# Depthwise convolution of a hybrid trunk kernel: two of four channel tiles as 32-column matmuls, and half of the softmax scaling on VectorE

## The chip, the cores and the metric

One core of one Trainium2 chip. The metric is the device time of one execution in microseconds (us). Engines are named as in the profile: PE is TensorE, PEld its weight loads, DVE is VectorE, ACT is ScalarE, POOL is GpSimd, SP is the engine that issues most DMAs.

## The reference

A two-layer trunk over 384 tokens (128 context tokens, then 256 latent tokens) of width 1024. Each layer is a half-step SwiGLU FFN, token mixing, a half-step SwiGLU FFN. The change touches only the token mixing of layer 0, the even mixer:

```python
q, k, v, a = split(h @ w_in)
q, k = rms_norm(q), rms_norm(k)            # rotary on latent tokens
attn = block_attention(q, k, v)            # 8 heads, 2 key/value heads, head size 64
glu  = a[..., :512] * sigmoid(a[..., 512:])
conv = silu(layer_norm(depthwise_conv(glu, conv_w, conv_b)))   # 31 taps, 512 channels
return concatenate([attn, conv]) @ w_out
```

The depthwise convolution gives each of 512 channels its own 31 weights: out[channel, n] is the sum over k of w[channel, k] times glu[channel, n + k - 15]. Context tokens attend to 128 keys, latent tokens to 384.

## The kernel before

Channels stand on the 128 partitions, tokens run along the free dimension (`TOK` = 384). A weight unit is 128 x 2048 f32 (1 MB); SP loads it into a ring of four, ACT makes its rounded high part (L515), DVE the rest (L837), and PE multiplies it in three passes, high by high, high by low, low by high (L1357 to L1359). FFNs take most of the time. A second ring, `m_raw`, carries 128 x 1024 rows of the modulation weights during the FFNs; in the even mixer it is idle.

The order of work is written out by hand, one program per engine, tied together by semaphores. In the even mixer the 512 convolution channels are four tiles `j` of 128 (`CT` = 4). `glu_mul(j)` on DVE writes the gated input of a tile into `padded[:, j, :]`, with zeros around both token groups, so that one tap is a multiplication of 399 columns (`CONV_N`) shifted by k. The parts that matter:

- **Taps on DVE.** `taps(j, k0, k1)` (L1111 for the first tap, L1115 for the others) adds one tap after the other into `conv[:, j, :]`; each waits for the one before it in the same tile. Tile 0 is done during the projections, tile 1 has 9 taps there and the rest later, tile 2 and 6 taps of tile 3 come in the attention loop, five taps a step, taken in turn from two tiles (`more_taps`).
- **Taps on PE.** The other 25 taps of tile 3 are matmuls (`conv_taps`, L1660) of a 128 x 128 diagonal matrix of weights by 399 columns of `padded`, summed in PSUM bank 1. ACT makes each diagonal (`tap_diags`, L647).
- **The attention loop** has 12 steps `m` (`PAIR_STEPS`): pairs of heads by three token blocks. Every third step, m = 0, 3, 6, 9, is a context block with 128 keys, the others are latent blocks with 384. I call them narrow and wide steps. In a step, PE makes the scores (L1671), DVE takes the maximum (L1193) and its scaled negative (L1195), ACT the exponential and its sum for both heads (L726), DVE the reciprocal (L1200), ACT scales the probabilities of both heads (L736), PE transposes them (`flip`, L1683), ACT copies them out of PSUM (`flipped_copy`, L716), and PE multiplies them by the values (L1694). After every third step a pair of heads is complete: ACT writes its high part (`mix_high`, L706) and DVE its low part (`mix_low`, L1204).
- **The orders in a step m.** PE: `scores(m + 2)` (waits for the exponential of m), taps, `values(m - 1)` (waits for the copies of m - 1), `flip(m)` (waits for the scaled probabilities of m). ACT: exponential of m, `mix_high` when due, the copies of m - 1, the scaling of m, one tap diagonal while there are any. DVE: reciprocal of m, `mix_low` when due, the maximum of m + 1, five taps.
- After the loop DVE adds the four tiles' sums into `conv_sum()` (L1235 to L1241), from which PE takes the mean for the layer norm (L1715), beside the output projection of the attention half (`proj_out`). That projection begins right after the last `values`.

Of the kernel before, what the change touches and what calls it, by code (L numbers as in the profile page):

```python
# [26 lines left out]
P = 128  # L27
# [22 lines left out]
DVE_TILES = CT - 1  # L50
DIAGS = 21
LAST_DVE_TAPS = 6
# [124 lines left out]
def build(nc, cache_k, cache_v, c, c_ctx, sgu_w, sgu_b, k_ident, k_rope, k_fourier, w_units, w_pairs, w_rows,  # L177
          x_cols, cond_cols, cols_a, cols_b, conv_cols, sgu_rows, y_cols, new_cache_k, new_cache_v):
    ctx = ExitStack()
    with ctx:  # L180
# [22 lines left out]
        conv_wt = sb("conv_wt", [P, CT, CONV_K])  # L203
        cond = sb("cond", [P, KT, COND_ROWS])
        cond_raw = sb("cond_raw", [P, 2 * KT])
        mod_pick = sb("mod_pick", [P, 2])
# [30 lines left out]
        tap_diag = sb("tap_diag", [P, DIAGS, P], stack=r)  # L237
        padded = sb("padded", [P, CT, PAD_N], stack=r)
# [82 lines left out]
        diag_ready, tap_used = sem("diag_ready"), sem("tap_used")  # L321
# [22 lines left out]
        def conv_sum():  # L344

            return rot[:].rearrange("p a b -> p (a b)")[:, 0:CONV_N]
# [7 lines left out]
        def row_products():  # L354
            return mod_rows(TRING + 2)

# [5 lines left out]
        def _(sp):  # L362
# [16 lines left out]
            def load_ffn(s):  # L379
                u0, n = UNIT0[s], TILE0[s]  # L380

                if s == 0:
# [8 lines left out]
                    for dst, src in ((vec_b[:], cols_b), (conv_wt[:], conv_cols)):  # L391
                        sp.dma_start(dst, src).then_inc(vectors_in, 16)
# [42 lines left out]
            for n in range(5, M0_UNITS):  # L435
                load_unit(u + n)
            load_ffn(2)
# [24 lines left out]
        def _(pool):  # L462
# [22 lines left out]
            pool.wait_ge(e_zero, 4)  # L485
            def add_channel_squares(m, sq):
# [16 lines left out]
        def _(act):  # L503
# [138 lines left out]
            def tap_diags(k0, k1):  # L642

                for k in range(k0, k1):
                    if k >= DIAGS + LAST_DVE_TAPS:
                        act.wait_ge(tap_used, k - DIAGS - LAST_DVE_TAPS + 1)
                    nc.scalar.activation(tap_diag[:, k % DIAGS, :], ident[:], ACT.Copy,  # L647
                                         scale=conv_wt[:, CT - 1, k:k + 1]).then_inc(diag_ready, 1)
# [22 lines left out]
            tap_diags(LAST_DVE_TAPS, LAST_DVE_TAPS + 6)  # L671
# [16 lines left out]
            tap_diags(LAST_DVE_TAPS + 6, LAST_DVE_TAPS + DIAGS)  # L688
# [29 lines left out]
            for m in range(PAIR_STEPS):  # L718
# [106 lines left out]
        def _(dve):  # L825
# [232 lines left out]
            nc.vector.tensor_reduce(mod_pick[:], ident[:].rearrange("p (a b) -> p b a", a=4)[:, 0:2, :], axis=AX.X,  # L1058
# [39 lines left out]
            dve.wait_ge(vectors_in, 32)  # L1098
# [34 lines left out]
            dve.wait_ge(vectors_in, 32)  # L1133
# [43 lines left out]
            taps(1, 0, 2)  # L1177
# [4 lines left out]
            taps(1, 2, 9)  # L1182
# [23 lines left out]
            last = CT - 1  # L1206
            rest = [1, 2] * (CONV_K - 9) + [2, last] * LAST_DVE_TAPS + [2] * (9 - LAST_DVE_TAPS)
            at = {1: 9, 2: 0, last: 0}

            def more_taps(n):  # L1210

                for j in rest[:n]:
                    taps(j, at[j], at[j] + 1)
                    at[j] += 1
                del rest[:n]

            dve.wait_ge(glu_done, 3)
            split(u + 8)
            more_taps(6)
# [11 lines left out]
            assert not rest  # L1231

            dve.wait_ge(conv_done, DVE_TILES)
            dve.wait_ge(dve_self, tap_at[last])
            a = mark(nc.vector.tensor_tensor(conv_sum(), conv[:, 0, :], conv[:, 1, :], ALU.add))  # L1235
            dve.wait_ge(tap_used, CONV_K - LAST_DVE_TAPS)
            b = mark(nc.vector.tensor_tensor(conv[:, last, :], conv[:, last, :], ps[:, 1, 0:CONV_N], ALU.add))
            dve.wait_ge(dve_self, a)
            dve.wait_ge(dve_self, mark(nc.vector.tensor_tensor(conv_sum(), conv_sum(), conv[:, 2, :], ALU.add)))
            dve.wait_ge(dve_self, b)  # L1240
            nc.vector.tensor_tensor(conv_sum(), conv_sum(), conv[:, last, :], ALU.add).then_inc(conv_summed, 1)  # L1241
# [110 lines left out]
        def _(pe):  # L1352
# [69 lines left out]
            def mod_columns(k):  # L1422
# [4 lines left out]
                for q in range(PAIR_TILES):  # L1427
                    ins = mm(ps[:, 7, 2 * q:2 * q + 2], mod_part[:, k % 2, q * P:(q + 1) * P], mod_pick[:], start=True, stop=True)
# [223 lines left out]
            tap = [LAST_DVE_TAPS]  # L1652

            def conv_taps(n):

                for k in range(tap[0], min(tap[0] + n, CONV_K)):
                    pe.wait_ge(diag_ready, k - LAST_DVE_TAPS + 1)
                    if k == LAST_DVE_TAPS:
                        pe.wait_ge(glu_done, CT)
# [229 lines left out]
```

## Time and profile before

| | |
|---|---|
| median of 3 runs | 1400.91 us (1400.43 to 1401.33) |
| the profiled execution, its own time | 1400.48 us |
| its span, first to last instruction | 1398.6 us |
| PE busy | 1383.6 us, 99% |
| DVE busy | 982.6 us, 70% |
| ACT busy | 566.0 us, 40% |
| POOL busy | 43.0 us, 3% |

The span is what the rows of the trace cover; the execution's own time is 1.9 us longer. Busy time is a mean over stages, and an engine with idle time in one stage can be the bound of the next, so the stage that changes has to be looked at by itself.

### The profile page before, as it was taken

What the parts mean: (1) busy time and instruction counts of PE and PEld (TensorE: products, weight loads), DVE (VectorE), ACT (ScalarE), POOL (GpSimd) and SP (SyncE); (2) the same over time, 40 slices, a digit from 0 to 9 for tenths busy, and PEclk for the clock granted to TensorE, in tenths of its full rate; (3) what the DMA queues carried; (4) which work ended last, traced back from release to release, by engine and by line L of the source; (5) the groups of instructions that cost most, each with busy time, mean ns of one, the idle gap of its engine ahead of it and who ended that gap; (6) DMA issues with size and microseconds to landing.
All of it is one profiled execution on the core that took longest, in us unless ns stands there. A gap on an engine that the chain in (4) does not pass through costs nothing.

```text
span 1398.6 us, 21118 instructions
## 1 busy us (share of the span) xinstructions
PE 1383.6 (99%) x8057; PEld 1347.5 (96%) x8057; DVE 982.6 (70%) x1502; ACT 566.0 (40%) x797; POOL 43.0 (3%) x48
## 2 busy tenths in 40 slices
PE   7999999999999999999999999999999999999999
PEld 6999999999958999999999999999999999999999
DVE  5788879849896988788338888787385488444422
ACT  4433332236586643333226333332365363333320
POOL 0000000010001200000002000000010110000000
PEclk8999999999999999999999999999999999999999
DMA  9865567533301365564334666574333253333331
GB/s 378 311 232 213 210 231 262 198 121 104 114 11 61 142 250 212 222 230 177 120 122 179 225 230 230 215 243 166 133 121 143 91 210 122 132 136 135 136 122 74
DMA packets 46373, 243.53 MB, mean 174 GB/s; under 512 B 5616, under 2 KB 8304, under 8 KB 25712
## 3 DMA queue, kind: packets, MB, share of 16 engines
q1 hardware_dynamic: 46032, 242.68, 48.0%
q8 instruction: 34, 0.56, 0.2%
q14 instruction: 19, 0.16, 0.0%
q10 hardware_dynamic: 288, 0.13, 0.0%
HBM read 241.09 MB, written 1.70 MB: 174 GB/s over the span
## 4 chain that ended last, share of the span: by engine, by line
PE 95%; DVE 3%; ACT 1%; issue 0%; DMA 0%; SPq 0%; DVEq 0%; ACTq 0%
PE ps L1357 30%; PE ps L1359 30%; PE ps L1358 30%; DVE conv L1115 1%; PE ps L1660 1%; PE ps L1814 0%; PE ps L1434 0%; PE ps L1765 0%; PE ps L1766 0%; PE ps L1767 0%; PE ps L1789 0%; DMA x<-in_x_cols 0%; DVE smax L1193 0%; PE ps L1418 0%; DVE n_full L915 0%
## 5 line engine op out<-in xcount | busy, mean ns | idle before, releaser
L1357 PE MATMUL ps<-a_hi,w_hi 128*128 128x384 f32 x1584 | 532.9, 336 | 0.5 <-DVE a_lo L923 0.4
L1358 PE MATMUL ps<-a_lo,w_hi 128*128 128x384 f32 x1584 | 529.6, 334 | 0.0
L1359 PE MATMUL ps<-a_hi,w_lo 128*128 128x384 f32 x1584 | 529.6, 334 | 0.0
L837 DVE TENSOR_TENSOR w_lo<-w_raw,w_hi 128x2048 fp32r<-128x2048 f32 x153 | 350.6, 2293 | 190.7 <-ACT w_hi L515 190.7
L515 ACT ACTIVATE w_hi<-w_raw 128x2048 fp32r<-128x2048 f32 x153 | 291.9, 1909 | 245.3 <-DMA w_raw<-in_w_units 245.1
L1357 PEld LDWEIGHTS ps<-a_hi,w_hi 128*128 128x128 f32 x1584 | 297.6, 188 | 6.4 <-issue 3.0
L859 DVE SCALAR_TENSOR_TENSOR m_raw<-m_raw 128x1024 f32<-128x1024 f32 x256 | 299.3, 1220 | 0.0
L1358 PEld LDWEIGHTS ps<-a_lo,w_hi 128*128 128x128 f32 x1584 | 297.7, 188 | 0.1
L1359 PEld LDWEIGHTS ps<-a_hi,w_lo 128*128 128x128 f32 x1584 | 297.6, 188 | 0.0
L1359 PE MATMUL ps<-h_hi,w_lo 128*128 (+1 forms) x704 | 236.6, 336 | 0.0
L1357 PE MATMUL ps<-h_hi,w_hi 128*128 (+1 forms) x704 | 236.5, 336 | 0.0
L1358 PE MATMUL ps<-h_lo,w_hi 128*128 (+1 forms) x704 | 236.5, 336 | 0.0
L594 ACT ACTIVATE glu<-ps 128x384 f32<-128x384 f32 x82 | 40.2, 491 | 282.0 <-PE ps L1359 282.0
L1359 PEld LDWEIGHTS ps<-h_hi,w_lo 128*128 128x128 f32 x704 | 132.4, 188 | 0.0
L1357 PEld LDWEIGHTS ps<-h_hi,w_hi 128*128 128x128 f32 x704 | 132.3, 188 | 0.0
L1358 PEld LDWEIGHTS ps<-h_lo,w_hi 128*128 128x128 f32 x704 | 132.3, 188 | 0.0
L1002 DVE TENSOR_TENSOR glu<-glu,ps 128x384 f32<-128x384 f32 x82 | 45.1, 550 | 75.4 <-ACT glu L594 75.4
L596 ACT ACTIVATE h_hi<-glu 128x384 f32 (+1 forms) x82 | 43.1, 526 | 131.0 <-DVE glu L1002 131.0
L1005 DVE TENSOR_TENSOR h_lo<-glu,h_hi 128x384 f32 (+1 forms) x82 | 45.8, 559 | 66.5 <-ACT h_hi L596 66.5
L541 ACT ACTIVATE a_hi<-n_full,m_shift 128x128 fp32r<-128x128 f32 x96 | 42.4, 455 | 43.9 <-DVE n_full L915 43.9
L1115 DVE SCALAR_TENSOR_TENSOR conv<-padded,conv_wt,conv 128x399 f32<-128x399 f32 x95 | 56.5, 631 | 1.3
L896 DVE SCALAR_TENSOR_TENSOR x<-ps,m_gate,x 128x128 f32<-128x128 f32 x96 | 34.6, 412 | 26.5 <-PE ps L1359 26.4
(193 smaller groups left out, 859.0 us busy)
## 6 DMA issues: line engine op xcount, KB each, us to landing
w_raw<-in_w_units SPq DMA_DIRECT2D x153, 1024.0 KB, 4.9
m_raw<-in_w_rows SPq DMA_DIRECT2D x128, 512.0 KB, 5.7
m_raw<-in_w_pairs SPq DMA_DIRECT2D x5, 1024.0 KB, 13.5
p_raw<-in_w_pairs SPq DMA_DIRECT2D x3, 1024.0 KB, 24.5
x<-in_x_cols SPq DMA_DIRECT2D x2, 768.0 KB, 5.3
out<-x SPq DMA_DIRECT2D x8, 192.0 KB, 1.9
fourier<-in_k_fourier SPq DMA_DIRECT2D x1, 768.0 KB, 8.1
m_raw<-in_c_ctx SPq DMA_DIRECT2D x1, 512.0 KB, 9.0
```

The source lines that it names most:

```text
L515: nc.scalar.activation(w_hi[:, slot(u), :], w_raw[:, slot(u), :], ACT.Copy).then_inc(hi_done, 1)
L541: nc.scalar.activation(a_hi[:, d, lo:hi], n_full[:, d, lo:hi], ACT.Identity, bias=m_shift[:, n, d, cnd:cnd + 1]).then_inc(a_hi_done, 1)
L594: nc.scalar.activation(glu[:, 0, :], ps[:, 2 * b, 0:TOK], ACT.Silu).then_inc(silu_done, 1)
L596: nc.scalar.activation(h_hi[:, bass.ds(t + RING * i, 1), :], glu[:], ACT.Copy).then_inc(h_hi_done, 1)
L837: nc.vector.tensor_tensor(w_lo[:, slot(u), :], w_raw[:, slot(u), :], w_hi[:, slot(u), :].bitcast(FP32), ALU.subtract).then_inc(lo_done, 1)
L859: nc.vector.scalar_tensor_tensor(out, mod_rows(n % TRING), 1.0, cond_row(cnd), ALU.mult, ALU.mult, accum_out=mod_cols[:, bass.ds(FIRST_TIL ...
L1002: nc.vector.tensor_tensor(glu[:, 0, :], glu[:, 0, :], ps[:, 2 * b + 1, 0:TOK], ALU.mult).then_inc(prod_done, 1)
L1005: nc.vector.tensor_tensor(h_lo[:, bass.ds(t + RING * i, 1), :], glu[:], h_hi[:, bass.ds(t + RING * i, 1), :].bitcast(FP32), ALU.subtract). ...
L1115: ins = nc.vector.scalar_tensor_tensor(conv[:, j, :], padded[:, j, k:k + CONV_N], conv_wt[:, j, k:k + 1], conv[:, j, :], ALU.mult, ALU.add)
L1357: mm(out, whi, mhi, start=start, stop=False)
L1358: mm(out, whi, mlo, start=False, stop=False)
L1359: return mm(out, wlo, mhi, start=False, stop=stop)
```

## The change

- Tiles 1 and 3 of the convolution go to PE completely; tiles 0 and 2 stay on DVE. PE takes four taps at a time (a quad; 8 quads a tile, the 32nd tap has weight zero). For that the input of the tile is copied by 16 DMAs into two free slots of `m_raw`: partition 32 k + c of group g holds channel 32 g + c shifted by k columns. A matmul with a 128 x 32 weight (four diagonals of 32, one above the other) then sums four taps of 32 channels. Four such matmuls, one for each group, fill the 128 partitions of the result (`conv_quads_of`).
- POOL makes all these weights once per tile before the attention (`quad_w`), ACT's diagonals (`tap_diags`) go away, and ACT takes each finished tile out of PSUM with its bias (`quad_evict`, in steps 4 and 11).
- In the attention loop PE has 4 quads ahead of the first step and then 1, 1, 1, 1, 0, 2, 1, 1, 1, 1, 1, 1 of them. DVE has tile 2 alone: 7 taps ahead of the loop, three a step for m < 3, then two.
- The probabilities of a step's first head are scaled on ACT as before, those of the second on DVE (`scale_second`), between the reciprocal and `mix_low` or the next maximum. `flip` waits for each half separately.
- The sums of the four tiles are added in another order: two additions in step 10, one after the loop. They stand in `padded[:, 0]` instead of `rot`.
- SP: 16 DMAs behind the loads of units 8 and 10 of this mixer. One small load of weights (`quad_wt`) at the start; DVE waits for three vector loads instead of two. `mod_pick` has 32 columns instead of 2.

```diff
-DVE_TILES = CT - 1
-DIAGS = 21
-LAST_DVE_TAPS = 6
+COND_GROUP = 32
+DVE_TILES = 2
+QUADS = 8
+GROUPS = 4
+PAD_W = PAD_N + 1
+QUAD_N = PAD_W - (P // COND_GROUP - 1)
...
+        def quad_x(i):
+            return m_raw[:, i, 0:GROUPS * QUAD_N].rearrange("p (g n) -> p g n", g=GROUPS)
+
+        def quad_w(i):
+            return m_raw[:, 2, i * UNIT // 2:(i + 1) * UNIT // 2].rearrange("p (q c) -> p q c", c=COND_GROUP)
...
             for n in range(5, M0_UNITS):
                 load_unit(u + n)
+                if n not in QUAD_LOAD:
+                    continue
+                i = QUAD_LOAD.index(n)
+                j = QUAD_TILES[i]
+                sp.wait_ge(glu_done, j + 1)
+                for k in range(P // COND_GROUP):
+                    for g in range(GROUPS):
+                        sp.dma_start(quad_x(i)[k * COND_GROUP:(k + 1) * COND_GROUP, g, :],
+                                     padded[g * COND_GROUP:(g + 1) * COND_GROUP, j, k:k + QUAD_N]).then_inc(quad_in[i], 16)
...
+            for i in range(CT - DVE_TILES):
+                nc.gpsimd.tensor_tensor(quad_w(i),
+                                        mod_pick[:].unsqueeze(1).to_broadcast([P, GROUPS * QUADS, COND_GROUP]),
+                                        quad_wt[:, i].rearrange("p g q -> p (g q)").unsqueeze(2)
+                                        .to_broadcast([P, GROUPS * QUADS, COND_GROUP]), ALU.mult).then_inc(quad_ready, 1)
...
-            def tap_diags(k0, k1):
...
+            def quad_evict(i):
+                j = QUAD_TILES[i]
+                act.wait_ge(quad_used, QUADS * (i + 1))
+                nc.scalar.activation(conv[:, j, :], ps[:, 1, 0:CONV_N], ACT.Identity,
+                                     bias=vec_b[:, B_CONV_B + j:B_CONV_B + j + 1]).then_inc(quad_out, 1)
...
                 act.wait_ge(rec_done, m + 1)
-                for h in range(2):
-                    n = 2 * m + h
-                    ins = nc.scalar.activation(probs(m)[:, h, 0:width(m)], probs(m)[:, h, 0:width(m)], ACT.Copy,
-                                               scale=srec[:, n:n + 1])
-                ins.then_inc(prob_done, 1)
-                k = LAST_DVE_TAPS + DIAGS + m
-                tap_diags(k, min(k + 1, CONV_K))
+                nc.scalar.activation(probs(m)[:, 0, 0:width(m)], probs(m)[:, 0, 0:width(m)], ACT.Copy,
+                                     scale=srec[:, 2 * m:2 * m + 1]).then_inc(prob_done, 1)
+                if m in QUAD_OUT:
+                    quad_evict(QUAD_OUT.index(m))
...
+            def scale_second(m):
+                width = CTX if m % TT == 0 else LAT + PAST
+                dve.wait_ge(rec_done, m + 1)
+                nc.vector.tensor_scalar(probs(m)[:, 1, 0:width], probs(m)[:, 1, 0:width], srec[:, 2 * m + 1:2 * m + 2], None,
+                                        ALU.mult).then_inc(half_scaled, 1)
...
             for m in range(PAIR_STEPS):
                 reciprocals(m)
+                scale_second(m)
                 if m >= 4 and (m - 4) % TT == 0:
                     mix_low((m - 4) // TT, ps[:, 0, 0:TOK])
                 if 1 <= m < PAIR_STEPS - 1:
                     attention(m + 1)
-                more_taps(5)
...
+                k = 7 + 2 * m + min(m, 3)
+                taps(2, min(k, CONV_K), min(k + 2 + (m < 3), CONV_K))
+                if m == PAIR_STEPS - 2:
+                    dve.wait_ge(conv_done, DVE_TILES)
+                    a = mark(nc.vector.tensor_tensor(conv_sum(), conv[:, 0, :], conv[:, 2, :], ALU.add))
+                    dve.wait_ge(dve_self, a)
+                    dve.wait_ge(quad_out, 1)
+                    a = mark(nc.vector.tensor_tensor(conv_sum(), conv_sum(), conv[:, 1, :], ALU.add))
...
+            def conv_quads_of(n):
+
+                for k in range(quad[0], quad[0] + n):
+                    i, q = k // QUADS, k % QUADS
+                    if q == 0:
+                        pe.wait_ge(quad_in[i], 16 * GROUPS * (P // COND_GROUP))
+                        pe.wait_ge(quad_ready, i + 1)
+                        if i:
+                            pe.wait_ge(quad_out, i)
+                    for g in range(GROUPS):
+                        ins = mm(ps[g * COND_GROUP:(g + 1) * COND_GROUP, 1, 0:CONV_N], quad_w(i)[:, g * QUADS + q, :],
+                                 quad_x(i)[:, g, 4 * q:4 * q + CONV_N], start=q == 0, stop=q == QUADS - 1)
+                    ins.then_inc(quad_used, 1)
+                quad[0] += n
...
             scores(0)
             scores(1)
-            conv_taps(3)
+            conv_quads_of(QUADS_AT[0])
             for m in range(PAIR_STEPS):
                 if m + 2 < PAIR_STEPS:
                     scores(m + 2)
-                conv_taps(2 if m < PAIR_STEPS - 2 else 1)
+                conv_quads_of(QUADS_AT[1 + m])
...
+QUADS_AT = [4, 1, 1, 1, 1, 0, 2, 1, 1, 1, 1, 1, 1]
+QUAD_OUT = [4, 11]
+QUAD_TILES, QUAD_LOAD = [1, 3], [8, 10]
```

## Rows read from the trace of the kernel before

**Rows 1.** The page: the chain that ended last, by engine.

```profile
PE 95%; DVE 3%; ACT 1%; issue 0%; DMA 0%; SPq 0%; DVEq 0%; ACTq 0%
```

**Rows 2.** Projections and loop: stretch, length, busy PE, PEld, DVE, ACT, POOL; clock, DMA.

```profile
316.00:381.30 65.30, 65.30 (x381) 63.22 (x380) 57.97 (x91) 38.18 (x67) 1.76 (x4) 1.00 0.31 106
381.30:428.67 47.37, 43.44 (x268) 23.81 (x267) 44.26 (x98) 39.03 (x107) 0.00 (x0) 1.00 0.07 23
```

**Rows 3.** The chain within 381 to 429 us, by line.

```profile
by line: DVE conv L1115 33.2%; PE ps L1660 17.5%; DVE smax L1193 8.6%; PE ps L1683 6.8%; PE ps L1671 6.2%; PE ps L1694 6.0%; ACT prob_t L716 3.4%; issue 2.4%; ACT e_sig L736 2.1%; DVE a_lo L1204 2.1%; DVE smaxn L1195 2.0%; ACT e_sig L726 1.
```

**Rows 4.** Timeline of DVE, steps 4 and 5: start, us, instruction, count, idle before.

```profile
398.46 0.56 DVE L1204 TENSOR_TENSOR a_lo<-ps,a_hi 128x384 fp32r<-128x384 f32 x1
398.94 0.95 DVE L1193 TENSOR_REDUCE smax<-ps 128x2 f32<-128x768 f32 x1
399.92 0.16 DVE L1195 SCALAR_TENSOR_TENSOR smaxn<-smax,stat_row 128x2 f32<-128x2 f32 x1
400.00 2.81 DVE L1115 SCALAR_TENSOR_TENSOR conv<-padded,conv_wt,conv 128x399 f32<-128x399 f32 x5
402.73 0.16 DVE L1200 RECIPROCAL srec<-ssum 128x2 f32<-128x2 f32 x1
402.80 0.40 DVE L1193 TENSOR_REDUCE smax<-ps 128x2 f32<-128x256 f32 x1
```

**Rows 5.** Timeline of ACT in steps 2 to 5, and the end of step 10's exponentials.

```profile
391.26 1.12 ACT L736 ACTIVATE prob<-prob,srec 128x384 f32<-128x384 f32 x2
392.29 0.39 ACT L647 ACTIVATE tap_diag<-ident,conv_wt 128x128 f32<-128x128 f32 x1
392.58 0.44 ACT L726 ACTIVATE e_sig<-ps,smaxn,stat_row 128x128 f32<-128x128 f32 x1
...
397.31 0.21 ACT L726 ACTIVATION_READ_ACCUMULATOR prob<-ps,smaxn,stat_row 128x1 f32 x1
...
400.12 0.67 ACT L726 ACTIVATE e_sig<-ps,smaxn,stat_row 128x384 f32<-128x384 f32 x1 [0.35 <-DVE smaxn L1195]
...
401.34 0.20 ACT L726 ACTIVATION_READ_ACCUMULATOR e_sig<-ps,smaxn,stat_row 128x1 f32 x1
401.43 0.86 ACT L716 ACTIVATE prob_t<-ps 128x384 f32<-128x384 f32 x2
...
419.96 0.20 ACT L726 ACTIVATION_READ_ACCUMULATOR prob<-ps,smaxn,stat_row 128x1 f32 x1
```

**Rows 6.** Timeline of PE in step 5.

```profile
401.59 0.92 PE L1671 MATMUL ps<-kdup,qk 64*128 64x384 f32 x4 [0.19 <-ACT e_sig L726]
402.43 1.61 PE L1660 MATMUL ps<-padded,tap_diag 128*128 128x399 f32 x4
403.97 0.88 PE L1694 MATMUL ps<-prob_t,v_nat 128*64 128x128 f32 x12
404.78 0.88 PE L1683 MATMUL ps<-ident,e_sig 128*128 128x128 f32 x6
```

**Rows 7.** Timeline of PE at the kernel's start: matmuls with 32 weight columns.

```profile
31.44 1.07 PE L1418 MATMUL ps<-p_raw,cond 128*32 128x256 f32 x16
32.44 0.44 PE L1357 MATMUL ps<-a_hi,w_hi 128*128 128x384 f32 x1
```

**Rows 8.** DVE: two scaling groups by form, and taps of one tile alone.

```profile
L1298 DVE TENSOR_SCALAR o_v<-o_v,stat 128x512 f32<-128x512 f32 x3 | 1.3, 482 | 0.0
...
L1259 DVE TENSOR_SCALAR e_diag<-ident,stat 128x128 f32<-128x128 f32 x3 | 0.7, 285 | 0.0
...
368.71 4.65 DVE L1115 SCALAR_TENSOR_TENSOR conv<-padded,conv_wt,conv 128x399 f32<-128x399 f32 x7
```

**Rows 9.** POOL's additions (min/median/max ns), a 64 KB issue on SP, landing times.

```profile
L492 POOL TENSOR_TENSOR qk_sq<-qk_sq x3: 1015/1020/2873, 433.7 to 437.9; 128x384 f32<-128x384 f32 x3
...
326.03 0.65 SPq L434 DMA_DIRECT2D v_nat<-in_cache_v  x1
...
bs<-in_sgu_b SPq DMA_DIRECT2D x4, 64.0 KB, 8.1
```

More of the change, by code:

```diff
@@ L203, in build @@
         conv_wt = sb("conv_wt", [P, CT, CONV_K])
+        quad_wt = sb("quad_wt", [P, CT - DVE_TILES, GROUPS, QUADS])
         cond = sb("cond", [P, KT, COND_ROWS])
         cond_raw = sb("cond_raw", [P, 2 * KT])
-        mod_pick = sb("mod_pick", [P, 2])
+        mod_pick = sb("mod_pick", [P, COND_GROUP])
         mod_part = sb("mod_part", [P, 2, PAIR])
@@ L320, in build @@
         mix_hi, mix_ready = sem("mix_hi"), sem("mix_ready")
-        diag_ready, tap_used = sem("diag_ready"), sem("tap_used")
+        quad_in = [sem(f"quad_in{i}") for i in range(CT - DVE_TILES)]
+        quad_ready, quad_used, quad_out, half_scaled = (
+            sem(n) for n in ("quad_ready", "quad_used", "quad_out", "half_scaled"))
         ln_mean_done, ln_xc, ln_sq, ln_stat, ln_ms, ln_root, ln_diag, ln_bc, ln_y = (
@@ L390, in load_ffn @@
                     load_unit(u0 + 2)
[L391 removed]
+                    for dst, src in ((vec_b[:], cols_b), (conv_wt[:], conv_cols), (quad_wt[:], conv_quads)):
                         sp.dma_start(dst, src).then_inc(vectors_in, 16)
@@ L1204, in mix_low @@
                 nc.vector.tensor_tensor(a_lo[:, j, :], src, a_hi[:, j, :].bitcast(FP32), ALU.subtract).then_inc(mix_ready, 1)
[L1206 to L1215, printed above, removed]
+            split(u + 8)
             dve.wait_ge(glu_done, 3)
-            split(u + 8)
-            more_taps(6)
+            taps(2, 0, 7)
             glu_mul(3)
@@ L1229, in _ @@
                     attention(m + 1)
-                more_taps(5)
[L1231 to L1237, printed above, removed]
+                k = 7 + 2 * m + min(m, 3)
[6 more added lines that the diff above has]
+                    a = mark(nc.vector.tensor_tensor(conv_sum(), conv_sum(), conv[:, 1, :], ALU.add))
             dve.wait_ge(dve_self, a)
-            dve.wait_ge(dve_self, mark(nc.vector.tensor_tensor(conv_sum(), conv_sum(), conv[:, 2, :], ALU.add)))
-            dve.wait_ge(dve_self, b)
-            nc.vector.tensor_tensor(conv_sum(), conv_sum(), conv[:, last, :], ALU.add).then_inc(conv_summed, 1)
+            dve.wait_ge(quad_out, 2)
+            nc.vector.tensor_tensor(conv_sum(), conv_sum(), conv[:, 3, :], ALU.add).then_inc(conv_summed, 1)
             mix_low(QT - 1, ps[:, 0, 0:TOK])
@@ L1427, in mod_columns @@
                 for q in range(PAIR_TILES):
-                    ins = mm(ps[:, 7, 2 * q:2 * q + 2], mod_part[:, k % 2, q * P:(q + 1) * P], mod_pick[:], start=True, stop=True)
+                    ins = mm(ps[:, 7, 2 * q:2 * q + 2], mod_part[:, k % 2, q * P:(q + 1) * P], mod_pick[:, 0:2], start=True, stop=True)
                 ins.then_inc(cols_done, 1)
@@ L1650, in _ @@
             pe.wait_ge(e_tc, 2)
[L1652 to L1659, printed above, removed]
-                    mm(ps[:, 1, 0:CONV_N], tap_diag[:, k % DIAGS, :], padded[:, CT - 1, k:k + CONV_N], start=k == LAST_DVE_TAPS,
-                       stop=k == CONV_K - 1).then_inc(tap_used, 1)
-                    tap[0] = k + 1
+            quad = [0]
+            def conv_quads_of(n):
[11 more added lines that the diff above has]
+                quad[0] += n
             def scores(m):
@@ L1679, in flip @@
                 for h in range(2):
+                    if h:
+                        pe.wait_ge(half_scaled, m + 1)
+                    else:
+                        pe.wait_ge(prob_done, m + 1)
                     if m:
@@ L1709, in _ @@
             values(PAIR_STEPS - 1)
-            assert tap[0] == CONV_K
+            assert quad[0] == QUADS * (CT - DVE_TILES)
             def means(src, at):
@@ L1877 @@
     named["sgu_rows"] = np.ascontiguousarray(np.concatenate([vectors["sgu_norm_g"], vectors["sgu_norm_b"]]))
+    taps = np.zeros((QUADS * 4, CONV_CH), np.float32)
+    taps[:CONV_K] = np.asarray(inputs["conv_w"])[0]
+    quads = taps.reshape(QUADS, 4, CT, GROUPS, COND_GROUP).transpose(1, 4, 2, 3, 0).reshape(P, CT, GROUPS, QUADS)
+    named["conv_quads"] = np.ascontiguousarray(quads[:, QUAD_TILES])
     arrays, args = {}, []
```

26 lines of the change are left out of this document (9 added, 17 removed).

## The prediction

> **What bounds the kernel now.** I read the page first. Its chain by engine [rows 1] shows a kernel that is PE from end to end, so work taken from DVE or ACT is worth something only where PE waits for them. I looked for that place next, with the busy times by stretch [rows 2]. In the projections, 316 to 381.3 us, PE is busy for all of 65.3 us: the 9 taps of tile 1 and the diagonals that leave that stretch give nothing back. In the attention loop, 381.3 to 428.67 us, PE has 3.9 us without work and DVE is busy for 44.3 of 47.4 us. The chain within it [rows 3] has DVE's taps as its largest line, a third, with the maximum behind them, and PE's taps second. So the loop is set by DVE, and PE is not far behind.
>
> The timelines give the loop's pace. The exponentials of step 4 end at 397.52 and those of step 10 at 420.16 [rows 5]: 22.6 us for six steps, 11.3 for three. DVE's five taps take 2.73 us a step, 402.73 minus 400.00 [rows 4], 8.2 for three; three reciprocals (0.07 each), two wide and one narrow maximum with its negative (1.06 and 0.52, from 398.94 to 400.00 and from 402.80 and the next 0.12) and `mix_low` (0.48) are 3.3. Together 11.5, the whole pace: DVE has no gap. PE, by the starts of step 5 [rows 6]: scores 0.84, taps 1.54, values 0.81, flip 0.81, 4.0 us for a wide step and about 2.7 for the narrow one, 10.7 for three.
>
> **The change, part by part.**
>
> *Taps leave DVE.* Two instead of five a step. They are now of one tile, and seven in a row of one tile stand 0.66 apart (4.65 / 7) [rows 8] against 0.55 in turn. Two cost 1.3 us. They stand behind the maximum of m + 1 and are hidden by the exponentials of m + 1, which take 1.42 us (400.12 to 401.54) [rows 5]. Behind a narrow one (0.97: two halves, each shorter by 0.67 - 0.44 = 0.23) 0.3 us stick out.
>
> *Scaling of the second half on DVE.* A scaling of 512 columns takes 0.48 us and one of 128 columns 0.285 [rows 8], so 384 take about 0.41, and the next instruction starts about 0.07 sooner, after 0.34. Bounds: 0.2 (narrow) and 0.48. It stands between the reciprocal and the next maximum, in DVE's chain. ACT saves 0.51 in a wide step (half of 392.29 - 391.26) and 0.29 for each diagonal in steps 0 to 3 [rows 5].
>
> *Quads on PE.* The trace has the same form: 16 passes (each f32 matmul is two) of 256 columns with 32 weight columns, in four column groups, done in 32.44 - 31.44 = 1.00 us [rows 7]. The taps' four passes of 399 columns take 1.54 us: at 0.83 ns a column a pass is 0.33, four are 1.33, and 0.2 is lost at the change of shape [rows 6]. At that rate 16 passes of 256 columns one after the other would be 3.4 us; in 1.00 us four must run at once: 4 x 0.21 = 0.85 plus 0.15. A quad is 8 passes of 399 columns, so 2 x 0.33 + 0.2 = 0.86 us. Bounds: 0.66 (nothing lost) and 2.9 (all eight in a row). I take 0.86, since the row differs only in its columns. The Trainium skill's page "TensorE: Matmul & The Clock Gate", section "Part 3: Packing small matmuls", reports 2.38 times for three column groups; at that share of the ideal a quad would be an estimated 1.04 us and the forecast 0.9 us later. Its page "TensorEngine Tiling (Array Packing)", section "Key Properties", says that a change of tiling mode drains the array, which speaks against 32-column blocks between others; but the number of changes stays, a quad block stands where a tap block stood.
>
> PE for three steps is then: scores 2.1, quads 2.6, values 2.0, flips 2.0, together 8.7 instead of 10.7.
>
> *Behind cover.* POOL's two weight instructions have 1024 columns; at 1.02 us for 384 [rows 9] that is 2.7 each, at 2.87 it is 7.7 each. They start once POOL has cleared its tiles, near 325, and end by 341; the quads start at 382.5. While both engines work DVE slows, at most some us in total, and PE has a whole unit of work ahead. Without that cover PE would wait as long as the split of a unit is late. SP: 16 issues of 0.65 us [rows 9] are 10.4 us. Those of tile 1 start when its input is there, about 363, and end by 373.5 plus a landing of at most 8.1, 381.6, just before the use at 382.5. Behind them in SP's queue is unit 9's load, due at 372.5 and needed after 428. Those of tile 3 start at 382.6, land by 401.1 at worst, and are used in step 5, near 400. The next load in the queue waits for a unit of the output projection anyway. `quad_evict` costs ACT 0.4 in steps 4 and 11, before copies that wait for flips. The small load at the start and the wider `mod_pick` (under 0.1 us) lie under DVE's wait for x. The reordered additions cost DVE 1.2 us in step 10 instead of 2.2 after step 11; both lie before the mean is wanted.
>
> **The new loop.** With its taps gone DVE no longer sets the pace by its sum (about 3.3 + 0.9 for the scalings + 3.9 = 8.1 for three steps); latencies do. From the end of step 4's exponentials (time 0), the longest way: reciprocal and scaling, 0.6; `mix_low`, 0.48; wide maximum and negative, 0.97 + 0.16; step 5's exponentials, 1.42 + 0.04. That is 3.7, and PE waits for it with the scores of step 7. Then PE: scores 0.9, two quads 1.53, values(4) 0.81, flip(5) 0.81, to 7.7 (0.05 a hand-over). ACT must copy that flip (second half 0.43), scale step 6 (0.29), and only then makes step 7's exponentials (1.42): 9.95. The other way round, DVE and ACT alone, is 3.7 + 2.2 (narrow) + 3.1 = 9.0. With one quad instead of two, as in the next period, PE's way gives 9.3. I use 9.9 and 9.5 (in the second the flips start late). Saved on six steps: 22.6 - 19.4 = 3.2.
>
> Head, up to step 4: ACT saves the half-scaling and the diagonal of step 0 (0.6), and steps 2 to 4 take 10.0 (the way above) instead of 10.6: 1.2. Tail, from the end of step 10's exponentials to 428.67, 8.5 us: 3.7 to step 11's exponentials, 0.3 behind the tap, then copies 0.8, half-scaling 0.6, flip 0.9, copies 0.8, values 0.8, 7.9: 0.6. Sum 3.2 + 1.2 + 0.6 = 5.0. What follows is PE work that starts when the loop ends, and moves with it whole. Of the profiled execution's 1400.48 that leaves 1395.5; the runs' median is 0.4 higher, so 1395.9.
>
> **Rivals.**
> 1. *The forecast*, saved 3.6 to 6.4, 1394.5 to 1397.3: 60%.
> 2. *PE's order does not get in the way*: the pace is DVE's and ACT's 9.0 in both periods, which adds 0.9 + 0.5 there, and as much again at most at head, tail and hand-overs; saved 6.4 to 7.9, 1393.0 to 1394.5. For it: PE's sum is 8.7. Against: two quads stand before a flip that the next exponentials wait for. 15%.
> 3. *Latency takes it back*: if each wide step costs 0.3 more (scaling at the 0.48 bound, quads at 1.04, ACT's two hand-overs), eight of them take 2.4, and with tile 3's data late by 1.1 the saving is 1.5; 1397.3 to 1399.9, of which the part above 1398.1 is no change that can be told. 15%, 8 of it below the mark. Here and below the mark is 0.2%, 2.8 us, what a measurement can tell.
> 4. *Column groups don't overlap*, slower. With the eight passes in a row a quad is 2.9 us. PE's other work in the loop is 4 x 6.1 = 24.4 us, 16 quads are 46: 70 instead of 47.4, 1423. It decides where PE's sum with the 3.9 us that it waits today reaches the old loop, at (47.4 - 24.4 - 3.9) / 16 = 1.2 us a quad. Against: the 1.00 us of [rows 7]. For: there the moving columns lie in one row of the buffer, and nothing else of the loop ran beside them. 4%.
> 5. *The clock falls*, slower: PE is busy for 35 of 42 us instead of 43 of 47. The granted clock was 1.00 (2.4 GHz) in the whole loop [rows 2]. At 1.2 GHz all of the loop's PE work would take up to 35 us more; a single short fall 2. 4%.
> 6. *The quads hardly matter and some unseen wait ends the loop at its old time* (a copy that starts late): within 0.2%. 2%.
>
> **How the numbers follow.** Faster by over 0.2%: 60 + 15 + 7 = 82%, and half of rival 5's small falls, 1: 83%. Within: 8 of rival 3, 2 of rival 6, 1 of rival 5: 11%. Slower: 4 + 2 = 6%. The range takes in rivals 1 and 2 whole and rival 3 but for its slow end: 1393.0 to 1399.3.
>
> **What would show it.** The loop from the first scores at 381.3 to the last values should take 42.4 us instead of 47.4, PE's busy time there 35 to 37. Eight passes of a quad: 0.8 to 0.9 from the scores' end to the next block, starts four at a time. Step 4's exponentials should end at 396.3, step 10's at 415.7. DVE should show idle time ahead of its reciprocals, with ACT's sums as the releaser. A wait of PE for DMA at 382 or 400, a second table load on ACT at `quad_evict`, or a granted clock under 1.00 in the loop would make the forecast wrong.

## The result and the profile after

The changed kernel takes 1402.59 us (median of 20 runs, 1401.31 to 1405.29) against 1400.79 of 20 runs of the kernel before taken beside them: a ratio of 1.0015 [1.0009, 1.0021]. The forecast was 1395.9. So the time did not fall by 5 us; it rose by nearly 2, less than the 0.2% that the prediction took for its mark. Below, "before" and "after" are the two profiled executions: spans 1398.6 and 1399.9 us, granted clock 0.995 and 0.998.

I went first to the loop, with the busy times by stretch of after: start and end, length, then busy PE, PEld, DVE, ACT, POOL, clock, DMA. The first line is the stretch of [rows 2], the second the loop itself, from its first scores to the next unit's first pass.

```profile
381.30:428.67 47.37, 42.31 (x375) 23.12 (x374) 36.82 (x88) 36.64 (x98) 0.00 (x0) 1.00 0.14 42
382.13:424.21 42.08, 37.02 (x345) 18.28 (x345) 34.35 (x80) 33.18 (x93) 0.00 (x0) 1.00 0.16 47
```

Before, the loop ran from 381.3 to 428.67, 47.4 us; now it takes 42.1. The 42.4 of the forecast was right. PE is busy for 37.0 of them, DVE for 34.4. The timeline of PE in after shows the parts (start, us, what; "x8" is the passes of one quad, a row's time runs to the end of its last pass):

```profile
382.13 1.14 PE L1693 MATMUL ps<-kdup,qk 64*128 64x128 f32 x8
383.20 2.89 PE L1681 MATMUL ps<-m_raw 128*32 128x399 f32 x32
386.02 0.92 PE L1693 MATMUL ps<-kdup,qk 64*128 64x384 f32 x4
386.87 0.88 PE L1681 MATMUL ps<-m_raw 128*32 128x399 f32 x8
387.67 0.44 PE L1708 MATMUL ps<-ident,prob 128*128 128x128 f32 x2
...
423.40 0.88 PE L1719 MATMUL ps<-prob_t,v_nat 128*64 128x128 f32 x12 [0.69 <-ACT prob_t L742]
424.21 0.44 PE L1374 MATMUL ps<-a_hi,w_hi 128*128 128x384 f32 x1
```

From start to next start, four quads take 386.02 - 383.20 = 2.82 us and one 387.67 - 386.87 = 0.80: two groups of four passes that run at once, as [rows 7] had it. PE waits for no transfer here. DVE's timeline shows what has become of it:

```profile
404.35 1.30 DVE L1138 SCALAR_TENSOR_TENSOR conv<-padded,conv_wt,conv 128x399 f32<-128x399 f32 x2
406.90 0.17 DVE L1221 RECIPROCAL srec<-ssum 128x2 f32<-128x2 f32 x1 [1.25 <-ACT e_sig L752]
407.10 0.42 DVE L1226 TENSOR_SCALAR e_sig<-e_sig,srec 128x384 f32<-128x384 f32 x1
```

It idles 1.25 us ahead of a reciprocal, with ACT's sums as the releaser, where it had no gap in [rows 4].

So 5.3 us were saved and the kernel is longer. A sum over three stretches of the two executions finds them: PE reached the loop 0.8 us later (382.13 against 381.3), the loop gave 5.3 back, and from the loop's end to the last instruction before needed 1398.6 - 428.67 = 969.9 us, after 1399.9 - 424.21 = 975.7, 5.8 more. Behind the loop the change leaves PE's work as it was (only the place of the sums that it reads is another), and of DVE's it touches the additions of these sums. The costliest groups of the page show where the 5.8 us are. Of before (busy us, mean ns of one | idle time ahead):

```profile
L1357 PE MATMUL ps<-a_hi,w_hi 128*128 128x384 f32 x1584 | 532.9, 336 | 0.5 <-DVE a_lo L923 0.4
L1358 PE MATMUL ps<-a_lo,w_hi 128*128 128x384 f32 x1584 | 529.6, 334 | 0.0
...
L1359 PE MATMUL ps<-h_hi,w_lo 128*128 (+1 forms) x704 | 236.6, 336 | 0.0
L1357 PE MATMUL ps<-h_hi,w_hi 128*128 (+1 forms) x704 | 236.5, 336 | 0.0
L1358 PE MATMUL ps<-h_lo,w_hi 128*128 (+1 forms) x704 | 236.5, 336 | 0.0
```

Of after:

```profile
L1374 PE MATMUL ps<-a_hi,w_hi 128*128 128x384 f32 x1584 | 532.9, 336 | 1.1 <-DVE a_lo L946 0.9
L1375 PE MATMUL ps<-a_lo,w_hi 128*128 128x384 f32 x1584 | 529.6, 334 | 0.0
...
L1374 PE MATMUL ps<-h_hi,w_hi 128*128 (+1 forms) x704 | 239.2, 340 | 0.0
L1375 PE MATMUL ps<-h_lo,w_hi 128*128 (+1 forms) x704 | 239.2, 340 | 0.0
L1376 PE MATMUL ps<-h_hi,w_lo 128*128 (+1 forms) x704 | 239.2, 340 | 0.0
```

The passes that stream `a_hi` and `a_lo` are the same to the nanosecond. Those that stream `h_hi` and `h_lo` (the second half of each FFN, 2112 of them) last 340 ns instead of 336 by these records. Passes overlap, so their cost is the time from start to start. Before's PE timeline in the last FFN:

```profile
1329.69 0.34 PE L1359 MATMUL ps<-h_hi,w_lo 128*128 x1
...
1335.41 0.34 PE L1359 MATMUL ps<-h_hi,w_lo 128*128 x1
```

And after's:

```profile
1330.02 0.34 PE L1375 MATMUL ps<-h_lo,w_hi 128*128 x1
...
1335.32 0.34 PE L1375 MATMUL ps<-h_lo,w_hi 128*128 x1
```

Between the two rows of before lie 33 steps, 173.3 ns each; between those of after 30, 176.7 ns each. 3.3 ns more on 2112 passes are 7.0 us, of which 1584 passes (5.3 us) lie behind the loop. About 0.5 us of the 5.8 stays without an account: in the runs below that have the change without the slow passes, the stretch behind the loop takes 970.1 to 971.0 us (e1, e5, e6, e14, e15) against 969.9 before.

The other 528 passes lie ahead of the loop and lose 1.8 us there, yet PE reached the loop only 0.8 later. The rest is chance of the two executions: after's first FFN pass began 0.5 us earlier (at 21.2 against 21.7), and before had a short fall of the clock at about 310 us that after did not have. The same stretch, first of before, then of after (the granted clock is the third number from the end):

```profile
300.00:316.00 16.00, 15.27 (x90) 14.42 (x90) 9.95 (x30) 7.16 (x16) 5.09 (x5) 0.89 0.39 133
300.00:316.00 16.00, 15.25 (x97) 14.22 (x95) 10.30 (x28) 6.99 (x18) 5.08 (x5) 1.00 0.37 133
```

In the slow groups no engine waits for another, clock and columns are the same, PE has no idle time. What differs is where the tensors stand. `quad_wt` (256 bytes a partition) and the wider `mod_pick` are allocated ahead of the region that `h_hi` and `h_lo` share with the attention's tensors, and move it from byte 157376 to 157728 of the partition.

### The profile page after: what moved, and what is told of

It reads as the page before. It is cut to its first block, busy times and chain, and to the rows that moved or that the text cites. A ratio compares the mean times of both kernels' runs of the same rounds, so it can differ in the third digit from the quotient of the medians.

```text
span 1399.9 us, 21260 instructions
## 1 busy us (share of the span) xinstructions
PE 1383.2 (99%) x8135; PEld 1348.0 (96%) x8135; DVE 970.9 (69%) x1476; ACT 553.7 (40%) x762; POOL 47.6 (3%) x50
## 4 chain that ended last, share of the span: by engine, by line
PE 95%; DVE 2%; DMA 1%; ACT 1%; SPq 0%; issue 0%; DVEq 0%; ACTq 0%
PE ps L1374 30%; PE ps L1375 30%; PE ps L1376 30%; DMA m_raw<-in_w_pairs 1%; PE ps L1839 0%; DVE conv L1138 0%; PE ps L1790 0%; PE ps L1792 0%; PE ps L1791 0%; PE ps L1719 0%; PE ps L1814 0%; PE ps L1435 0%; PE ps L1451 0%; PE ps L1681 0%; PE ps L1693 0%; DVE smax L1214 0%
## 5 line engine op out<-in xcount | busy, mean ns | idle before, releaser
L1374 PE MATMUL ps<-xt_hi,w_hi 128*128 128x386 f32 x128 | 44.3, 346 | 0.3 <-DVE xt_lo L965 0.2
```

The costliest lines, as they stand in the source:

```text
L1374: mm(out, whi, mhi, start=start, stop=False)
```

## The experiments

Addresses are bytes within a partition, taken from each built program. I give them modulo 256, that is, what is left over after the last multiple of 256. In both kernels `w_hi`, `w_lo`, `a_hi` and `a_lo` stand at 128; `h_hi` and `h_lo` at 192 before and at 32 after. First theory: the place of `h_hi`/`h_lo` makes the 7 us. Rival: the 5.8 us come from something else that the change leaves behind (DVE's or ACT's later order, a transfer).

**e1, the changed kernel with 32 bytes more ahead of `h_hi`** (192 became 32, now 64):

```diff
+        sb("pad", [P, 8])
         r = ExitStack()
         h_hi = sb("h_hi", [P, FT, TOK], F32R, r)
```

> The changed kernel with 32 bytes of unused room in front of the region of h_hi, so that h_hi starts 64 bytes further on from a multiple of 64 as it did before the change. Alignment theory: each of the 2112 FFN passes that stream h_hi or h_lo goes back from 0.1767 to 0.1733 us, 7.0 us in all; the attention loop keeps its 42.1 us. Then about 1395.6 us. Rival, that something else of the change (DMAs, POOL, clock) slows the FFNs: no difference, about 1402.6.

Measured: 1396.69 us (6 runs), ratio 0.9968 [0.9956, 0.9980]. Padding alone takes 5.9 us off the changed kernel (5.6 when each is set against the runs of before beside it).

**e2, the kernel before with the same 32 bytes** (192 became 224):

> The kernel before with the same 32 bytes of unused room and nothing else. Alignment theory: the FFN passes that stream h_hi and h_lo go from 0.1733 to 0.1767 us, about 1407.8 us, 7 us slower. Rival: no difference, about 1400.8.

Measured: 1407.10 us, ratio 1.0046 [1.0033, 1.0060]. Nothing of the change is in this kernel, and it pays 6.6 us: the loss is not the new loop's.

**e3, the changed kernel with 64 bytes** (96), which was to tell whether a remainder modulo 64 decides:

> The changed kernel with 64 bytes of unused room instead of 32: h_hi again starts 32 bytes past a multiple of 64. Alignment theory: as the changed kernel, 1402.6 us, passes at 0.1767. A theory in which the absolute place or the neighbours of the tensors matter and not the remainder by 64 would let it move too.

Measured: 1397.50 us, ratio 0.9978 [0.9968, 0.9987]; the passes took 173.4 ns. Here `h_hi` stands at 32 modulo 64, as in the slow kernels after and e2, and it is fast: a rule by 64 bytes of `h_hi`'s own place falls.

**e4, `h_lo` alone 32 bytes further in e1** (64 and 96):

> As the 32 byte version, with 32 more bytes of room between h_hi and h_lo, so that only h_lo starts 32 bytes past a multiple of 64. Alignment theory: only the passes that stream h_lo (one in three, 704) take 0.1767 us, 2.3 us more than the 32 byte version, about 1397.9. If the region as a whole mattered, it would be like one of the two, 1395.6 or 1402.6.

Measured: 1400.06 us, ratio 0.9997 [0.9988, 1.0006]. Either place is good by itself (e1, e3), the two together are not. The costliest groups of e4:

```profile
L1376 PE MATMUL ps<-h_hi,w_hi 128*128 (+1 forms) x704 | 238.6, 339 | 0.0
L1377 PE MATMUL ps<-h_lo,w_hi 128*128 (+1 forms) x704 | 238.0, 338 | 0.0
L1378 PE MATMUL ps<-h_hi,w_lo 128*128 (+1 forms) x704 | 236.9, 336 | 0.0
```

The passes that go from `h_hi` to `h_lo` or back are the dear ones; the one that is followed by another of `h_hi` costs hardly more. So how the tensors that PE reads in turn stand to each other matters. The second theory was: what counts is the distance modulo 256 between the streamed tensor and the weights (by itself it does not explain e4, where both distances are ones that e1 and e3 show to be free). Its rival, "theory A" in the expectations: each tensor's own place modulo 256, slow from 224 through 0 to 32.

**e8, the kernel before with `a_hi` and `a_lo` 32 bytes further** (8 floats ahead of `a_hi`, 56 behind `a_lo`, so that all else stands modulo 256 where it stood):

> The kernel before with 32 bytes of room before a_hi and 224 behind a_lo, so that only a_hi and a_lo move, from 128 to 160 by the remainder of their address by 256 bytes; h_hi, h_lo and the weights keep 192 and 128. Theory A (a remainder of about 224 to 32 by 256 in the streamed tensor is slow, the runs so far): 160 is outside, a_hi and a_lo passes stay at 0.1733 us, 1400.5. Theory B (any streamed tensor that is not on a multiple of 64 is slow): it fell with the run with 64 bytes, and would give 4752 passes x 3.3 ns, 1416.

Measured: 1404.96 us, ratio 1.0030 [1.0018, 1.0041]; 4752 passes of `a_hi` and `a_lo` at 174.5 ns instead of 173.5, those of `h_hi` and `h_lo` unchanged at 173.3. It is no matter of `h_hi` and `h_lo` alone, and theory A, which put 160 outside the slow places and expected 1400.5, missed.

**e10, the kernel before with everything 32 bytes further** (one pad ahead of `w_raw`):

> The kernel before with 32 bytes of room ahead of everything: all tensors, weights too, move by 32 bytes, and h_hi goes to remainder 224 by 256, the slow place of the run before with 32 bytes, while its distance to the weights stays. If the absolute place of the streamed tensor decides, h passes take 0.1767 us and the time is 1407. If its distance to the weights decides, nothing changes: 1400.5.

Measured: 1400.53 us, ratio 0.9998 [0.9989, 1.0008]. `h_hi` stands at 224 as in e2, and e2's 6.6 us are gone, now that the weights have moved with it: against theory A, and as the distance has it.

**e11 and e12, the changed kernel with 224 and 192 bytes** (`h_hi` at 0 and 224):

> The changed kernel with 224 bytes of room: h_hi at remainder 0 by 256, a multiple of every power of two up to 256. Theory A: 0 lies between 224 and 32, both slow, so slow: 1402.6. A theory by which a rounder address is better: 1396.5.

> The changed kernel with 192 bytes of room: h_hi at remainder 224 by 256, as the kernel before with 32 bytes of room was. Theory A, by the remainder by 256: slow, 1402.6. If what made that kernel slow was its address by 512 or more, it may be fast: 1396.5.

Measured: 1401.97 us, ratio 1.0008 [0.9999, 1.0018], passes at 176.0 ns; and 1403.21 us, ratio 1.0014 [1.0005, 1.0024], 176.7 ns. Both are slow, which either theory allows; a rounder address is no better.

**e9, the kernel before with `w_hi` alone 32 bytes further** (all behind it moves by 256):

```diff
         w_lo = sb("w_lo", [P, RING, UNIT], F32R)
+        sb("pad_a", [P, 8])
         w_hi = sb("w_hi", [P, RING, UNIT], F32R)
+        sb("pad_b", [P, 56])
```

> The kernel before with w_hi alone moved up by 32 bytes; w_lo, a_hi, a_lo, h_hi and h_lo stand where they stood. If what decides is the distance modulo 256 between the streamed operand and the weights, passes of h with w_hi stand at +32 now and take about 1 ns more each, passes of a with w_hi at -32 stay at 173.3 ns: +0.7 to +1.5 us, ratio 1.0005 to 1.001, and the passes with w_lo keep their time. If the streamed operand's own place decides, nothing changes. If the weights' own place decides, passes of both a and h with w_hi change alike.

Measured: 1415.48 us, ratio 1.0107 [1.0092, 1.0123], ten to twenty times the 0.7 to 1.5 us that were expected. The costliest groups of e9:

```profile
L1361 PE MATMUL ps<-a_hi,w_lo 128*128 128x384 f32 x1584 | 538.3, 340 | 0.0
L1360 PE MATMUL ps<-a_lo,w_hi 128*128 128x384 f32 x1584 | 536.3, 339 | 0.0
L1359 PE MATMUL ps<-a_hi,w_hi 128*128 128x384 f32 x1584 | 533.8, 337 | 0.1
...
L1361 PE MATMUL ps<-h_hi,w_lo 128*128 (+1 forms) x704 | 239.0, 339 | 0.0
```

The dearest passes are those with `w_lo`, which did not move and stands to `a_hi` and `h_hi` as before. The pass behind each of them uses `w_hi`, and its weights are loaded meanwhile. The second theory as it stood did not foresee this; a third was tried: the distance of the streamed tensors to the weights, and besides it a price for `w_lo` and `w_hi` (or `h_hi` and `h_lo`, e4) standing apart modulo 256. For the passes of `h_hi` and `h_lo` e9 bears it out: their distances to the two weight tensors are 32 and 64, both free where the weights stand alike (e14 below, and before), and yet they take 175.6 ns.

**e16, the same with `w_hi` 64 bytes further**:

> The kernel before with w_hi alone moved by 64 bytes: its distance to a_hi is 192 modulo 256 and to h_hi 128, and w_lo stands 64 from it. If only the distance of streamed tensor to weights counts, passes of a with w_hi stay at 173.3 ns and passes of h with w_hi take about 2.7 ns more (1408 passes, 3.8 us): about 1404.5 us. If w_lo and w_hi standing apart costs by itself, as the passes beside a change of weights in e9 say, it costs here too: 10 us or more over before. If apart by 64 is harmless as 64 is between h and the weights, and the distance to h is no matter either, it is before's time.

Measured: 1412.67 us, ratio 1.0078 [1.0064, 1.0092], 11.6 us. The expectation has a slip: `w_hi` and `h_hi` both stand at 192 here, so their distance is 0 and not 128, and its 3.8 us for those passes have no ground. The time lies in its second branch all the same, since 8.9 us of it are on the passes of `a_hi` and `a_lo` (175.4 ns instead of 173.5). But the slow steps are others than in e9. The costliest groups of e16:

```profile
L1359 PE MATMUL ps<-a_hi,w_hi 128*128 128x384 f32 x1584 | 539.0, 340 | 0.1
L1361 PE MATMUL ps<-a_hi,w_lo 128*128 128x384 f32 x1584 | 536.0, 338 | 0.0
L1360 PE MATMUL ps<-a_lo,w_hi 128*128 128x384 f32 x1584 | 529.6, 334 | 0.0
```

From start to start the dearest step, 177.3 ns, goes from one pass of `w_hi` to the next, and the one from `w_hi` to `w_lo` is free at 173.1; in e9 the steps that change the weight tensor were the dear ones (178.2 and 175.9). So that moving `w_hi` away from `w_lo` costs is measured at two distances. It is not shown that each change of the weight tensor carries the cost. Nor is it shown how much of it `a_hi` would pay for its distance to `w_hi` alone, since no run has it 192 or 224 from both weight tensors.

**e13 and e14, the changed kernel with 256 and 128 bytes** (`h_hi` at 32 and 160):

> The change with 256 bytes of padding ahead of h_hi. If the effect repeats by 256 bytes, this is the changed kernel's time, 1402.6 us, and its passes of h take 340 ns each by the records. If it repeats by 512 or not at all, the time is another one, down to e1's 1396.7 us.

> The change with 128 bytes of padding ahead of h_hi: distance to the weights 32 modulo 256, the weights where they were. If the distance decides, as e15: about 1 ns a pass over e1, about 1398.8 us. If h's own place (160 modulo 256) decides, nothing is known of it; by its remainder modulo 128 it would be as the changed kernel's, 1402.6 us.

Measured: 1402.48 us, ratio 1.0010 [1.0001, 1.0019], 176.7 ns, the changed kernel's time; and 1396.87 us, ratio 0.9970 [0.9961, 0.9979], 173.3 ns. At the one place where it was asked, the effect repeats by 256 bytes. At a distance of 32 the passes of `h_hi` cost nothing; the 1 ns carried over from e8 was wrong for them.

**e15, new tensors first**. `quad_wt` and `mod_pick` are allocated ahead of the weights; `h_hi` and `h_lo` stand exactly where the changed kernel has them, at 157728, and the weights have moved to 0 modulo 256. One quad stands in the last step as in e6 below.

```diff
+        quad_wt = sb("quad_wt", [P, CT - DVE_TILES, GROUPS, QUADS])
+        mod_pick = sb("mod_pick", [P, COND_GROUP])
         r = ExitStack()
         w_raw = sb("w_raw", [P, RING, UNIT], stack=r)
...
-        quad_wt = sb("quad_wt", [P, CT - DVE_TILES, GROUPS, QUADS])
...
-        mod_pick = sb("mod_pick", [P, COND_GROUP])
```

> e6's order of quads without padding; quad_wt and mod_pick stand ahead of everything, so that weights, a_hi and a_lo move by 384 bytes and h_hi and h_lo stay exactly where the changed kernel has them, at 157728. Distance to the weights modulo 256 is 32 then. If the distance decides, the passes of h cost about 1 ns more than at 192 (as a_hi's did at 32), 2112 of them 2 us: about 1398.4 us. If h's own place decides, they take the 176.7 ns that they have there in the changed kernel: about 1402.5 us. Passes of a_hi and a_lo stay at 173.4 ns by the distance, their own place has changed from 128 to 0 modulo 256.

Measured: 1395.26 us (5 runs), ratio 0.9963 [0.9950, 0.9977], the lowest time of the study. The timeline of e15 in the last FFN:

```profile
1329.78 0.34 PE L1376 MATMUL ps<-h_hi,w_lo 128*128 x1
...
1330.65 0.34 PE L1375 MATMUL ps<-h_lo,w_hi 128*128 x1
```

Five steps of 174 ns, 173.3 over all passes, against 176.7 at the same address in after. A tensor's own place is not it. (In e10 and e15 `a_hi`, `x` and `m_raw` moved along with the weights. These passes read none of the three, but no run moved the two weight tensors alone, so that it is the distance to the weights is in so far argued.)

The runs in which `w_lo` and `w_hi` stand alike, and `h_hi` and `h_lo` too, worked out from all starts of such passes in each trace; the distance is the place of `h_hi` less that of the weights:

```
distance mod 256   ns a pass of h   places of h and weights, runs
 32                173.3            160, 128 (e14); 32, 0 (e15)
 64                173.3            192, 128 (before, e8); 224, 160 (e10)
 96                176.7            224, 128 (e2, e12)
128                176.0            0, 128 (e11)
160                176.7            32, 128 (after, e13)
192                173.3            64, 128 (e1)
224                173.4            96, 128 (e3)
```

The passes of `h_hi` and `h_lo` cost 2.7 to 3.4 ns more where the distance is 96 to 160, and at most 0.1 at 32 or 64 either way. A distance of 0 was not run for them; `a_hi` and `a_lo` stand at 0 in before, with 173.5 ns.

The last three runs ask about the loop, all without the slow passes.

**e5, the quads alone**: e1 with both heads' scaling back on ACT.

```diff
-                nc.scalar.activation(probs(m)[:, 0, 0:width(m)], probs(m)[:, 0, 0:width(m)], ACT.Copy,
-                                     scale=srec[:, 2 * m:2 * m + 1]).then_inc(prob_done, 1)
+                for h in range(2):
+                    n = 2 * m + h
+                    ins = nc.scalar.activation(probs(m)[:, h, 0:width(m)], probs(m)[:, h, 0:width(m)], ACT.Copy,
+                                               scale=srec[:, n:n + 1])
+                ins.then_inc(prob_done, 1)
...
-                scale_second(m)
...
```

> The change with 32 bytes of padding ahead of h_hi (as e1, which took 1396.7 us), and with both heads' scaling back on ACT: the quads alone. If the loop is bound by DVE and PE as the prediction had it, ACT's two scalings (0.41 us each, eight to nine of them more) come back ahead of PE's attention values: 0.5 to 1.5 us over e1, about 1397.7 us, ratio 0.997 to 0.998. If the scaling on DVE was what gave the loop its time, it is 2.5 us or more over e1, at 1399.2 us or above. If it was worth nothing, the time is e1's within 0.3 us.

Measured: 1396.92 us, ratio 0.9971 [0.9959, 0.9983], and its loop takes 42.0 us. The scaling on DVE is worth nothing beside the quads.

**e6, no pair of quads before the end**: e1 with `QUADS_AT = [4, 1, 1, 1, 1, 0, 1, 1, 1, 1, 1, 1, 2]`.

> e1 with one of the two quads of one step moved to the last step, so that no step but the last issues two. If PE's order is on the path where two quads stand together (1.48 us ahead of the attention values), the time falls by 0.3 to 0.7 us under e1, to about 1396.2 us; if PE waits there anyway for ACT, it stays at e1's 1396.7 us; if the last step's extra quad delays the convolution's reading, it rises by 0.7 us.

Measured: 1396.32 us, ratio 0.9966 [0.9954, 0.9978]. Against e1 that is inside the spread of the runs, but its loop takes 41.4 us in the trace, as e15's does, where every other version with quads and a clock of 1.00 takes 42.0 to 42.1. The chain of after shows why, PE from 400.63 on without a gap (the first row is start, us, what):

```profile
400.63 0.92 PE ps L1693 x4
401.54 1.48 PE ps L1681 x16
403.02 0.81 PE ps L1719 x12
403.83 0.81 PE ps L1708 x6
```

In e6 the quad block in that place is half as long, and the chain is shorter by its 0.67:

```profile
400.82 0.92 PE ps L1694 x4
401.73 0.81 PE ps L1682 x8
402.54 0.81 PE ps L1720 x12
403.35 0.81 PE ps L1709 x6
```

**e7, the scaling alone**: the kernel before with `scale_second` on DVE and its five taps a step.

> The kernel before with one head's scaling on DVE and its taps unchanged. DVE bounds the loop before (44.3 of 47.4 us busy), so twelve more scalings there, most at 0.41 us, would add 3.5 to 4.7 us less what ACT's shorter chain gives back: 1403.0 to 1404.5 us, ratio 1.002 to 1.003. If ACT's chain was the bound instead, the time falls by 1 us or more. No address moves against the kernel before, so nothing of it is the streamed passes'.

Measured: 1405.34 us, ratio 1.0033 [1.0021, 1.0045], its loop 51.6 us. DVE's timeline of e7 has no idle time ahead of its reciprocal, unlike after's:

```profile
393.52 2.81 DVE L1113 SCALAR_TENSOR_TENSOR conv<-padded,conv_wt,conv 128x399 f32<-128x399 f32 x5
396.25 0.16 DVE L1198 RECIPROCAL srec<-ssum 128x2 f32<-128x2 f32 x1
396.44 0.29 DVE L1203 TENSOR_SCALAR e_sig<-e_sig,srec 128x128 f32<-128x128 f32 x1
396.65 0.95 DVE L1191 TENSOR_REDUCE smax<-ps 128x2 f32<-128x768 f32 x1
```

## Why the prediction was wrong

**What bounds the kernel: right.** DVE set the loop's pace and PE came next. e7 shows the first: each scaling put into DVE's chain comes out as time, 4.2 us of loop for twelve. Projections and FFNs are PE's alone.

**Quads on PE: right.** 0.80 us for one and 1.48 for two, forecast 0.86 and 1.53. [rows 7] was a fair stand-in although its moving columns lie otherwise. The 2.38 times for three column groups of the Trainium skill's page "TensorE: Matmul & The Clock Gate", section "Part 3: Packing small matmuls", from which an estimated 1.04 us was worked out, was too careful for four: rival 4 is dead. The drain of the array that the prediction set against the quads did not show as an extra cost: 0.80 less the 0.66 of two passes leaves 0.14, less than the 0.2 that the sum allowed.

**The new loop: right in size.** Forecast 5.0 saved and 42.4 us long, measured 5.3 and 42.1. Step 4's exponentials end at 396.95 (forecast 396.3), step 10's at 416.35 (415.7), both 0.7 late, and PE entered the loop 0.8 late; the six steps between took 19.4, as forecast. PE's order is in the way as rival 1 had it and rival 2 not: the pair of quads costs 0.67 (e6). One term was mis-placed inside the sum: the scaling's share. The prediction let ACT save it at head and tail and DVE pay for it; e5 shows the two cancel, so the taps alone made the gain.

**Behind cover, in the loop's region: right.** POOL's two weight instructions took 2.5 us each, estimated 2.7. The transfers of both tiles landed in time, with a median of 2.4 us over all 32 against the bound of 8.1, and PE waited for none.

**The step that failed** is in "Behind cover": "The small load at the start and the wider `mod_pick` (under 0.1 us) lie under DVE's wait for x", together with "What follows is PE work that starts when the loop ends, and moves with it whole". The two tensors were costed by the time of the instructions that fill them. That they take room, and that 352 bytes of room ahead of `h_hi` and `h_lo` change the speed of 2112 passes that the diff does not touch, was not in the sum at all. No rival had it: rivals 3, 4 and 6 put their losses into the loop, and rival 5 concerned the clock. The sum with the missing term, 5.3 saved in the loop less 7.0 on the passes, gives 1.7 us slower, and 1.8 was measured; that it comes so close is in part luck, since the 0.5 us behind the loop and the clock are not in it. Without the slow passes (e1) the kernel takes 1396.69 us, the forecast 1395.9. By its median e1 gains 3.8 us and not the loop's 5.3: about 0.5 goes behind the loop, and in some executions the clock takes more.

**Rival 5, the clock: seen, and small.** In after the granted clock is 1.00 through the loop. In the profiled execution of e3 it is not:

```profile
400.00:412.00 12.00, 11.08 (x90) 5.14 (x90) 8.51 (x21) 7.77 (x24) 0.00 (x0) 0.87 0.00 1
```

There the clock stood at its lower level (1.2 GHz) for a part of the 12 us. e3's loop took 43.5 us instead of 42.1, and so did e1's, with 0.93 from 400 to 424.2, and e12's took 43.6. That is a single short fall of about 1.4 us, where the prediction had said 2. It comes in some executions and not in others: in three of the eleven profiled executions with quads, in none of the seven without, while runs of e3 go from 1395.3 us, at a mean clock of 0.996, to 1399.8, at 0.993. Ahead of it, from 390 to 400, PE had been busy for 8.0 of 10 us in e3 and 9.0 in e1; in after it was 8.4 and the clock stayed up. So the loop with more idle time on PE pays for it now and then, and what decides in which execution stays open.

## What to carry to other kernels

A change that adds or widens a buffer moves every buffer allocated behind it, and a long stream of matmuls can feel that. Before costing such an edit at nothing, compare the addresses of streamed tensors and weights in the two built programs; keep tensors that TensorE reads in turn alike modulo 256 bytes, and the streamed ones at a distance from the weights that a run has shown to be free (here 0 for `a_hi`, 32 or 64 for `h_hi`). When a gain is missing, compare mean durations of the groups that the diff does not touch before looking for a wait: 336 against 340 ns in an untouched group, with no idle time, pointed at the missing 7 us here, and one pad of 32 bytes in each kernel (e1, e2) showed them to be the place's.

## What the runs showed of the hardware

- A pass with 128 x 128 weights over 384 f32 columns starts 173.3 ns after the last one where all stand well, 176.7 where the streamed tensor is 96 or 160 bytes (modulo 256) from the weights (176.0 at 128): 2%, over 2112 passes 7.0 us. The difference between the two is the addresses' alone (e10, e15). The Trainium skill's page "TensorE: Matmul & The Clock Gate", section "Back-to-back issue gap", gives N / 2.4 + 2.5 ns as the gap of isolated matmuls, from which 384 columns would take an estimated 162.5 ns, with no term for addresses; both values measured here are longer.
- Moving one of two weight tensors that are used in turn 32 or 64 bytes away from the other cost most: 14.8 us (e9) and 11.6 us (e16) on some 6900 passes, about 2 ns each. `h_hi` and `h_lo` 32 apart cost 2.2 ns a pass (e4).
- Open: why, and why the slow steps are different ones at 32 and at 64 bytes (e9, e16). At a distance of 32, passes of `a_hi` and `a_lo` cost 0.9 ns more (e8) and those of `h_hi` and `h_lo` nothing (e14, e15). The table holds for this kernel's FFN passes; what TensorE's reads collide in was not measured.
- The time of other engines on moved tensors did not show: the loops of after, e4, e11, e13 and e14 take 42.1 us each, with the shared region at five different places.
